# Beginning of a two-layer hybrid diffusion backbone: shift and scale in two column halves, tokens first

## What is computed

```
for l in range(DEPTH):                       # 2 layers
    mod_x = (silu(c) @ w_mod[l] + b_mod[l]); mod_c = (silu(c_ctx) @ w_mod[l] + b_mod[l])
    sh1, sc1, g1, sh2, sc2, g2 = split(mod_x, 6)          # csh1.. of mod_c alike
    hx = rms_norm(xs, norm_mix_g[l]) * (1 + sc1) + sh1;  hc = rms_norm(cs, norm_mix_g[l]) * (1 + csc1) + csh1
    oc, ox = even_mixer(hc, hx, w_in, ...) if l == 0 else odd_mixer(hc, hx, w_qkv, ...)
    xs = xs + g1 * ox;  xs = xs + g2 * sq_relu_mlp(rms_norm(xs) * (1 + sc2) + sh2, w1, w2)    # cs alike in layer 0
# even_mixer starts with h @ w_in; its first 1024 output columns are xr, which a short convolution and
# two gated scans use; then come yr, q/k/v, z and the gate columns
```

## Time and profile before

| | us |
|---|---|
| median of three runs (lowest, highest) | 1482.41 (1480.11, 1483.84) |
| the profiled execution's own time | 1480.53 |
| its span | 1478.7 |
| first product with a weight unit starts | 53.30 |

### The profile page before, as it was taken

The page is one execution under the profiler, slowest core; times in us unless marked ns, Lnnn a source line. Parts: engine busy times, 40 slices in busy tenths (PEclk is TensorE's granted clock), DMA queues, the critical chain, the costliest instruction groups (busy, mean ns, idle before and its releaser), DMA issues.

```text
span 1478.7 us, 22711 instructions
## 1 busy us (share of the span) xinstructions
PE 1400.7 (95%) x8312; PEld 1138.3 (77%) x8312; DVE 762.1 (52%) x1203; ACT 700.3 (47%) x1102; POOL 293.8 (20%) x291
## 2 busy tenths in 40 slices
PE   5799999989899999999999999999998998899998
PEld 2577777767678888877868888888887766899997
DVE  0744789875345555444364433344235545665664
ACT  2538888867434444432253421243125544554543
POOL 0100123333256666551300000000030000200001
PEclk9899999989999999999999999999999999999999
DMA  7542323221454333452323232333323320455653
GB/s 279 168 101 72 86 80 91 73 70 43 166 177 143 129 130 115 150 193 86 95 84 90 95 100 86 100 90 94 100 86 101 99 72 0 136 177 185 185 184 101
DMA packets 135695, 170.59 MB, mean 115 GB/s; under 512 B 11011, under 2 KB 122038, under 8 KB 135606
## 3 DMA queue, kind: packets, MB, share of 16 engines
q1 hardware_dynamic: 134720, 169.18, 36.4%
q10 hardware_dynamic: 886, 0.19, 0.1%
HBM read 168.30 MB, written 1.05 MB: 115 GB/s over the span
## 4 chain that ended last, share of the span: by engine, by line
PE 74%; ACT 8%; DVE 8%; issue 4%; DMA 3%; POOL 1%; ACTq 1%; SPq 0%; DVEq 0%; POOLq 0%
PE bank L1908 54%; PE bank L2208 3%; PE bank L2196 3%; PE bank L1866 2%; DMA raw<-in_w_mod 2%; ACT w_hi L779 2%; DVE w_lo L1330 2%; DVE qkv L1354 1%; PE bank L2225 1%; PE bank L2057 1%; PE bank L2150 1%; PE bank L2072 1%; POOL qkv L630 1%; PE bank L2174 1%; ACT l_i L1023 1%
## 5 line engine op out<-in xcount | busy, mean ns | idle before, releaser
L1330 DVE TENSOR_TENSOR w_lo<-raw,w_hi 128x1024 fp32r<-128x1024 f32 x216 | 269.4, 1247 | 458.7 <-ACT w_hi L779 458.6
L779 ACT ACTIVATE w_hi<-raw 128x1024 fp32r<-128x1024 f32 x216 | 228.6, 1058 | 462.5 <-PE bank L1908 458.3
L1908 PE MATMUL bank<-h_hi,w_hi 128*128 128x512 f32 (+1 forms) x1024 | 377.7, 369 | 21.1 <-ACT h_hi L967 8.0
L1908 PE MATMUL bank<-h_hi,w_lo 128*128 128x512 f32 (+1 forms) x1024 | 369.1, 361 | 0.0
L1908 PE MATMUL bank<-h_lo,w_hi 128*128 128x512 f32 (+1 forms) x1024 | 365.7, 362 | 1.2 <-DVE h_lo L1498 1.2
L1908 PEld LDWEIGHTS bank<-h_hi,w_hi 128*128 128x128 f32 x1024 | 195.0, 190 | 67.5 <-issue 23.0
L1908 PEld LDWEIGHTS bank<-h_lo,w_hi 128*128 128x128 f32 x1024 | 192.9, 190 | 36.0 <-issue 2.6
L1908 PEld LDWEIGHTS bank<-h_hi,w_lo 128*128 128x128 f32 x1024 | 194.8, 190 | 32.2
L1908 PE MATMUL bank<-hid_hi,w_hi 128*128 128x512 f32 (+1 forms) x512 | 172.8, 338 | 0.9 <-DVE w_lo L1330 0.6
L1908 PE MATMUL bank<-hid_hi,w_lo 128*128 128x512 f32 (+1 forms) x512 | 172.1, 336 | 0.0
L1908 PE MATMUL bank<-hid_lo,w_hi 128*128 128x512 f32 (+1 forms) x512 | 172.1, 336 | 0.0
(11 more groups left out here) (279 smaller groups left out, 2087.6 us busy)
## 6 DMA issues: line engine op xcount, KB each, us to landing
raw<-in_mlp_w SPq DMA_DIRECT2D x128, 512.0 KB, 3.6
raw<-in_w_mod SPq DMA_DIRECT2D x96, 512.0 KB, 4.5
raw<-in_even_w_in SPq DMA_DIRECT2D x48, 512.0 KB, 3.7
raw<-in_even_w_out SPq DMA_DIRECT2D x16, 512.0 KB, 3.4
raw<-in_attn_w_qkv SPq DMA_DIRECT2D x16, 512.0 KB, 3.5
raw<-in_attn_w_o SPq DMA_DIRECT2D x8, 512.0 KB, 3.4
xin<-in_ctx SPq DMA_DIRECT2D x1, 1024.0 KB, 9.2
xin<-in_x SPq DMA_DIRECT2D x1, 1024.0 KB, 11.3
```

The lines of the kernel that those rows point to most:

```text
L779: act.activation(w_hi[:, j % SPLIT], raw[:, j % RAW], ACT.Copy).then_inc(hi_ready, 1)
L1330: dve.tensor_tensor(w_lo[:, j % SPLIT], raw[:, j % RAW], w_hi[:, j % SPLIT].bitcast(F32), ALU.subtract).then_inc(split_done, 1)
L1908: return pe.matmul(bank[2 * pair + t][:, 0:T - n0], w[:, j % SPLIT, k, t * P:(t + 1) * P], x_[:, n0:T], start=(kk == 0 and first), stop=(k ...
```

## The change

Tokens are asked for first, in two column halves, each with its own semaphore. `w_mod` pieces of layer 0's shift and scale now hold 512 columns of shift and the same 512 of scale, so that the first eight pieces give both for feature tiles 0 to 3, the second eight for 4 to 7. They have eight slots of their own (`first_w`); the ninth and later wait on `mod_used`. Units of `xr` are asked for between them. The nineteen small loads are issued on POOL's queue. Copy, transposes, bias and gain are done per half (`half_copy`, `half_flip`, `evac_half`). PE first turns the tokens, then sums the squares with three products instead of eight (DVE adds tiles 0 to 5, `square_added`), then turns the small rows. The four first units are taken in the order pair 0, pair 1 (features 0 to 511), pair 0, pair 1 (features 512 to 1023), with the second eight pieces of `w_mod` between them. ACT writes `h_hi` itself; DVE computes gain times n_x plus shift once more in full precision (`n_y`) to get `h_lo`. POOL has no part in the first norm. DVE's softplus stands behind the norm. Of the constants, only identity, ones and epsilon come first.

```diff
@@ -520,23 +531,39 @@
 
             def load_first_mod(m):
 
-                k, col = m % KT, m // KT * MOD_COLS
-                sp.wait_ge(mod_used, m + 1)
-                sp.dma_start(raw[:, k % RAW].rearrange("p a c -> p (a c)"),
-                             a["w_mod"][0].rearrange("(k p) c -> k p c", p=P)[k][:, col:col + MOD_COLS]).then_inc(mod_in[k % RAW], 16)
+                k, col = m % KT, m // KT * (D // 2)
+                if m >= FIRST:
+                    sp.wait_ge(mod_used, PRIME_MOD + m - FIRST + 1)
+                sp.dma_start(first_w[:, m % FIRST].rearrange("p (g a) c -> p g (a c)", g=2),
+                             a["w_mod"][0].rearrange("(k p) (g c) -> k p g c", p=P, c=D)[k][:, 0:2, col:col + D // 2])\
+                  .then_inc(mod_first[m % FIRST], 16)
+
+            def load_first_unit(n):
+
+                pair, part = FIRST_PAIRS[n]
+                load_unit(w_dram["w_in"].rearrange("(h k p) c -> h p k c", p=P, k=UNIT_K)[part], n, n, pair * UNIT_C)
 
             sp.dma_start(rowsA[0:8, :], a["c_ctx"].rearrange("(k p) -> k p", p=P)).then_inc(s_c, 16)
             sp.dma_start(rowsA[8:16, :], a["c"].rearrange("a (k p) -> (a k) p", p=P)).then_inc(s_c, 16)
-            sp.dma_start(cst[:, 0:P], a["consts"][:, 0:P]).then_inc(s_c, 16)
-            for m in range(RAW):
+            sp.dma_start(cst[:, 0:N_FIRST], a["consts"][:, 0:N_FIRST]).then_inc(s_c, 16)
+            for half in range(2):
+                c_ = half * (D // 2)
+                for n, name in enumerate(("ctx", "x")):
+                    sp.dma_start(xin[:, 2 * n:2 * n + 2, c_:c_ + D // 2],
+                                 a[name][0].rearrange("(n p) d -> p n d", p=P)[:, :, c_:c_ + D // 2]).then_inc(s_x[half], 16)
+            for m in range(KT):
                 load_first_mod(m)
-            sp.dma_start(xin[:, 0:2, :], a["ctx"][0].rearrange("(n p) d -> p n d", p=P)).then_inc(s_x, 16)
-            sp.dma_start(xin[:, 2:4, :], a["x"][0].rearrange("(n p) d -> p n d", p=P)).then_inc(s_x, 16)
-            sp.dma_start(cst[:, P:N_EARLY], a["consts"][:, P:N_EARLY]).then_inc(s_ones, 16)
-            for m in range(RAW, 2 * MOD_BATCH):
+            load_first_unit(0)
+            for m in range(KT, KT + 3):
                 load_first_mod(m)
-            sp.dma_start(wg[:, :, :], w_dram["w_in"][:, 6144:6176].rearrange("(k p) c -> p k c", p=P)).then_inc(s_x, 16)
-            sp.wait_ge(mod_used, 2 * MOD_BATCH + PRIME_MOD)
+            load_first_unit(1)
+            for m in range(KT + 3, 2 * KT - 1):
+                load_first_mod(m)
+            load_first_unit(2)
+            load_first_mod(2 * KT - 1)
+            load_first_unit(3)
@@ -559,6 +586,8 @@
                                   it * (2 * UNIT_C) + (s["c0"] + pair * UNIT_C))
 
                 peeled = 0
@@ -582,11 +611,31 @@
         def _(pool):
             pool.memset(cs[:, :, 2:], 0.0).then_inc(s_cs, 1)
 
-            def first_norm():
-
-                for k in range(KT):
-                    pool.wait_ge(nrm["h"], 2 * (k + 1))
-                    pool.tensor_copy(h_hi[:, k], n_x[:, k]).then_inc(nrm["hi"], 1)
+            def rows(dst, r0, src, n):
@@ -722,7 +771,6 @@
                 glink(pool.tensor_copy(mix_hi[:, t_], xc[:, t_]))
                 pool.tensor_tensor(mix_lo[:, t_], xc[:, t_], mix_hi[:, t_].bitcast(F32), ALU.subtract).then_inc(g_x, 1)
 
-            first_norm()
             gate_parts()
             for i in range(22):
                 silu(i)
@@ -944,17 +999,21 @@
 
                 act.preload_act_table_set("natural_log_exp_and_others")
                 root("mix0", T)
-                mod_copy(0)
-
                 split_hi(0, 0)
-                split_hi(1, 1)
-                act.wait_ge(s_gain, 1)
-                for k in range(KT):
-                    act.wait_ge(nrm["t"], k + 1)
-                    for v, t0, t1 in SEGS:
-                        y_ = n_x[:, k, t0:t1]
-                        act.activation(y_, y_, ACT.Identity, bias=modv[:, 0, 0, k, v:v + 1],
-                                       scale=gain[:, 0, 0, k, v:v + 1]).then_inc(nrm["h"], 1)
+                for half in range(2):
+                    half_copy(half)
+                    act.wait_ge(s_gain, half + 1)
+                    for k in range(HALF * half, HALF * half + HALF):
+                        act.wait_ge(nrm["t"], k + 1)
+                        for v, t0, t1 in SEGS:
+                            ins = act.activation(h_hi[:, k, t0:t1], n_x[:, k, t0:t1], ACT.Identity, bias=modv[:, 0, 0, k, v:v + 1],
+                                                 scale=gain[:, 0, 0, k, v:v + 1])
+                        ins.then_inc(nrm["high"], 1)
+                        if k == KT - 2:
+                            split_hi(3, 3)
+                    if half == 0:
+                        split_hi(1, 1)
+                        split_hi(2, 2)
 
             def norm(name, layer, which, c0):
 
@@ -1458,19 +1492,53 @@
                 link(dve.scalar_tensor_tensor(out=gain[:, layer, which], in0=modv[:, layer, 3 * which + 1], scalar=1.0,
                                               in1=g_, op0=ALU.add, op1=ALU.mult))
 
+            def evac_half(half):
+
+                dve.wait_ge((half_t, mod_t)[half], 1)
+                for h in range(2):
+                    k0, k1 = HALF * half + h, HALF * half + HALF
+                    ps = bank[(X1, X2)[half]][:, h * P:h * P + P].rearrange("p (g i w) -> p g i w", g=2, i=2)[:, :, :, 0:2]
+                    b_ = V("b_mod", 0, 2 * KT).rearrange("p (g k) -> p g k", g=2)[:, :, k0:k1:2].unsqueeze(3).to_broadcast([P, 2, 2, 2])
+                    link(dve.tensor_tensor(modv[:, 0, 0:2, k0:k1:2, :], ps, b_, ALU.add))
+                k0 = HALF * half
+                g_ = V("mix_g", k0, HALF).unsqueeze(2).to_broadcast([P, HALF, 2])
+                link(dve.scalar_tensor_tensor(out=gain[:, 0, 0, k0:k0 + HALF], in0=modv[:, 0, 1, k0:k0 + HALF], scalar=1.0,
+                                              in1=g_, op0=ALU.add, op1=ALU.mult))
+                dve.sem_inc(s_gain, 1)
...
             def first_norm():
 
+                def scaled(k):
+                    dve.tensor_tensor(n_x[:, k], xT[:, k], n_rs[:, :], ALU.mult).then_inc(nrm["t"], 1)
+
+                def low(k):
+                    dve.wait_ge(nrm["t"], k + 1)
+                    for v, t0, t1 in SEGS:
+                        ins = dve.tensor_scalar(n_y[:, k, t0:t1], n_x[:, k, t0:t1], gain[:, 0, 0, k, v:v + 1],
+                                                modv[:, 0, 0, k, v:v + 1], ALU.mult, ALU.add)
+                    link(ins)
+                    dve.wait_ge(nrm["high"], k + 1)
+                    dve.tensor_tensor(h_lo[:, k], n_y[:, k], h_hi[:, k].bitcast(F32), ALU.subtract).then_inc(nrm["lo"], 1)
+
                 dve.wait_ge(nrm["rt"], 1)
-                for k in range(KT):
-                    dve.tensor_tensor(n_x[:, k], xT[:, k], n_rs[:, :], ALU.mult).then_inc(nrm["t"], 1)
-                evac_mod(0)
-                make_gain(0, 0)
-                dve.sem_inc(s_gain, 1)
+                scaled(0)
+                scaled(1)
                 split_lo(0, 0)
+                evac_half(0)
+                for k in range(HALF):
+                    low(k)
+                    if k + 2 < HALF:
+                        scaled(k + 2)
+                for k in range(HALF, KT):
+                    scaled(k)
                 split_lo(1, 1)
-                for k in range(KT):
-                    dve.wait_ge(nrm["hi"], k + 1)
-                    dve.tensor_tensor(h_lo[:, k], n_x[:, k], h_hi[:, k].bitcast(F32), ALU.subtract).then_inc(nrm["lo"], 1)
+                split_lo(2, 2)
+                evac_half(1)
+                dve.sem_inc(s_mod, 1)
+                for k in range(HALF, KT):
+                    low(k)
+                    if k == KT - 2:
+                        split_lo(3, 3)
...
+
+            def square_added(k):
+
+                dve.wait_ge(nrm["sq"], k + 1)
+                if k > 1:
+                    dve.wait_ge(s_acc, k - 1)
+                dve.tensor_tensor(n_sq[:, 0], n_sq[:, 0], n_sq[:, k], ALU.add).then_inc(s_acc, 1)
+
+            turned(1)
+            turned(3)
+            square_added(1)
+            square_added(2)
+            turned(5)
+            square_added(3)
+            square_added(4)
+            turned(7)
+            square_added(5)
...
+            first_norm()
             dve.wait_ge(s_lam, 2)
             softplus(64, 80)
             link(dve.tensor_scalar(lru_h, lru_c, -LRU_C / 2, None, ALU.mult))
             dve.tensor_scalar(lru_c, lru_c, -LRU_C, None, ALU.mult).then_inc(s_lam, 1)
-            first_norm()
...
+            def first_sum():
+
+                pe.wait_ge(s_acc, KT - 3)
+                pe.matmul(bank[X0][:, :], C("ones"), n_sq[:, 0], start=True, stop=False)
+                for k in (KT - 2, KT - 1):
+                    pe.wait_ge(nrm["sq"], k + 1)
```

(33 more changed lines are left out.)

170 lines of the change are left out of this document (97 added, 73 removed).

## The result

The changed kernel takes 1471.34 us (median of five, 1465.11 to 1474.42), the kernel before 1483.46 beside it: ratio 0.9912, 95% interval 0.9884 to 0.9941. Forecast were 1470 and a gain of 12.3; measured is 12.1. The profiled execution took 1474.42, the slowest of the five, with a span of 1472.6. The first weight product starts at 31.06 us instead of 53.30, the fifth unit at 65.94 instead of 77.2.

A forecast was written before the change was run, and what follows sets the result against it. TensorE, busy 95% of the span, was taken as the bound, so gains lie in its idle beginning: fifth unit 13.3 us earlier, less 1.0 for the clock, gain 12.3, giving 1468.2 profiled, 1470 against the median; range 1462 to 1478.

The forecast's parts named there:

- G: Time when the first half's gain is ready, at the kernel's beginning: R + 5.1 on VectorE, so 29.1 us.
- The step from G to the fifth unit: First four units of `xr`: VectorE paces, the fifth starts at G + 34.7, 63.8 us, after 3.2 us idle on TensorE.
- The small rows are the open term: Beginning: the small row loads, now issued by POOL, set the gain through R, taken as 24 us.
- R: Time when TensorE can read the small rows: 24 us, the middle between 19.5 and 28.
- lower bound: Earliest R: ACT's 18.4 us for 19 loads, counted from POOL's first free moment at 1.0, so 19.5 us.
- transposes, copies, squares and root run beneath the pieces: Beginning: with tokens landing near 8 and 10 us, this work is hidden under the `w_mod` pieces' transfers.
- The steps that I had put behind R: From the rows to the gain: 5.1 us on VectorE, 4.6 on TensorE, including 2.0 for seventh and eighth piece.
- The step on transfers: Beginning: at 405 GB/s from 7 us, the eighth piece is usable at about 20.9 us, the first weight unit at 22.2.
- Tensor-by-scalar: VectorE's `h_lo` tiles: each 256-column operation takes 0.27 us, between 0.24 and 0.49.
- The clock behind the gap: TensorE's 3.2 us idle ahead of the fifth unit costs clock speed: between 0 and 1.5 us, taken as 1.0.
- The rival in which TensorE stays at 1.2 GHz between tiles: First units: low clock while waiting for VectorE puts the fifth unit at 80.1 us, time 1485; chance 6%.
- Everything should move by the same amount: Behind the fifth unit all queues, waits and durations stay the same, so its 13.3 us earlier start carries through.

The follow-up runs named there:

- the first profile: The changed kernel as first measured, against the kernel before: 1471.34 us, ratio 0.9912; its profiled execution took 1474.42.
- the second profile: The changed kernel measured again with no edit, against the kernel before: 1467.26 us, ratio 0.9898.
- the run with tiles first: Changed kernel with TensorE turning all eight token tiles before the third piece, then two pieces, sum, rows, six pieces: 1467.25 us, ratio 0.9912 to the kernel before.

## Why the prediction was right, and where its steps were not

**The time was right, and its two main steps were right in size.** G came out at 29.73 for 29.1, the fifth unit at 65.94, 64.04 and 64.23 for 63.8. The step from G to the fifth unit was right in place too. TensorE, without a gap from 31.06, sets the second half's gain: at G + 19.6 in the first profile and 18.6 in the second, for 18.5. From there VectorE paces. Softplus stands in the 2.6 us gap ahead of the fifth unit (3.2 forecast), shown by moving it.

**But G was right for a wrong reason.** The step "The small rows are the open term" failed. R is 17.6 by the list of transfers after, 17.55 by the wait in the kernel before with that part alone, both below the "lower bound" of 19.5: I had laid ACT's whole 18.4 us over POOL's start, though POOL's issues need 0.48 to 0.68 each and rows landed 2.6 to 7.2 us after theirs, many in flight at once. Rows on ACT's queue change nothing either. The Trainium skill, DMA: Bandwidth & Descriptors (Queues, rings and completion order), says that a DMA engine takes packets from its queues in turn; by this small loads would not wait out a backlog on another queue, and I had put R near 20 by it. The 17.6 us on POOL's queue agree with it; the 10.4 us of the last load on ACT's queue, a queue of its own too, stay unexplained. Anatomy of one DMA in that page gives about 2.0 us fixed for a transfer issued by GpSimd; the first row's 2.6 us is near it, and the loads are not strung out: all 19 were over 16.3 us after the first issue.

What stood in place of R is the sentence "transposes, copies, squares and root run beneath the pieces". On their data they could; on TensorE's one queue they take turns, and the sum ended at 24.7. Had I added up that queue from its first tile, with its waits for pieces, I should have found it. So TensorE read the rows at 25.2. The steps that I had put behind R then follow: 4.5 us from there to G on VectorE, for 5.1. On TensorE's side the seventh and eighth piece took 1.07 us together, not the 2.0 taken for the half clock; VectorE's side ended later, so this cost nothing. The step on transfers was short too: 405 GB/s from 7 us on was taken from before, 346 and 332 came; the eighth piece is usable at 23.6 instead of 20.9, the first weight unit at 24.85 instead of 22.2 (seen where nothing else holds them, in the run with tiles first). Why the rate was lower is open. That pieces of 2 KB rows are slower as such is not what the later windows show: 395 GB/s from 28 to 35 us, with pieces and units in turn. What ruled, the sum at 24.7, and next the eighth piece and the first unit, happened to lie where I had put the rows, at 24: that G came out was luck.

**Tensor-by-scalar** was mis-sized: 0.73 for two, 0.37 each, for the 0.27 taken between 0.24 and 0.49. I had scaled 0.486 with columns: half the columns took three quarters of the time. Little of it counts. In the first half TensorE sets the pace; in the second three tiles make 0.6 of the 0.8 us by which the last `h_lo` came later behind the gain than forecast. The other 1.1 of the 1.5 us in the first profile lies ahead of that gain: TensorE stayed at half clock longer at the start, so that the first two pieces between the products took 1.87 us where they took 1.00 in the second profile. Softplus and what follows took 0.3 less than forecast.

**The clock behind the gap** was at the end of its 0 to 1.5: from 66.7 to 70.1 us products of the fifth unit came every 0.43 us, eight of them, 0.195 too long each: 1.5, where I took 1.0. The rival in which TensorE stays at 1.2 GHz between tiles did not come; 0.59 from 28 to 35 us is the half clock at the start, for which the sum had 1.5 us.

**"Everything should move by the same amount"** holds only on average. In the first profile the changed kernel is 11.3 us ahead at the fifth unit, 13.0 at 322 us, 8.3 at 762, 6.1 at the end; in its second 13.2, 15.5, 14.8 and 12.8. Part of the 13.0 at 322 us is chance as well: the kernel before ran at half clock for 12 us behind its stop, the changed kernel for 4.6. The losses behind 322 us go with the clock: the span's mean granted clock is 0.987 before, 0.985 in the first profile and 0.989 in the second, and of the changed kernel's 15 executions the slowest has 0.982 and the five fastest 0.989 to 0.992. That a forecast within 2 us of the median was met owes something to luck too, with single runs from 1464.8 to 1475.8.

**Without the interleaving almost nothing was left of the gain** (ratio 0.9991): tokens first, slots and the rows' queue shorten the start by 9.9 us, and the order by halves gives 9.1 of them back. But up to some 5 us of that are the place of one pair of transposes in that run, so how much of the 12 belongs to the interleaving alone, nearly all or about half, stays open.

## What to carry to other kernels

Add up each in-order engine from its first instruction before calling work "hidden beneath" transfers: what is independent in its data still stands in one queue. Where TensorE waits for transfers ahead of its first product, move duties that are not needed yet behind it: eight pieces cost 13.3 us ahead, between 1 and 5 between the units, where their transfers were over. When one duty is moved, look at what stays queued behind it: a pair of transposes left in place made VectorE wait 5.18 us. Look for the next limit within 2 or 3 us before moving work: here softplus alone and tiles alone moved the start but not the time beyond its noise, and only together, with the gain's chain ahead of the first unit, did they show.

## What the runs showed of the hardware

**Half clock behind a stop has no fixed length.** The stop near 297 us is 5.1 us in all twelve profiles without work in it. Behind it TensorE ran at half clock although it had work again: for 3 to 5 us in nine of them, 9 in one (the kernel before with rows on POOL), 12 in two (the kernel before, 310.7 to 322.7, and softplus moved). Between executions of one kernel the end moves by up to 10 us (1465.7 to 1475.8), more than most of these edits, and the slower ones have the lower mean clock. This one stop is not the main source: with work in it single runs still spread over 7.2 us.

**Transfers dip where the rows are issued by POOL.** Windows at 14 and 15 us, last column GB/s, of the changed kernel, and of the same with rows on ACT:

```profile
14.00:15.00 1.00, 1.00 (x8) 0.72 (x4) 0.00 (x0) 0.00 (x0) 0.00 (x0) 1.00 1.47 298
15.00:16.00 1.00, 1.00 (x9) 0.20 (x8) 0.00 (x0) 0.78 (x2) 0.00 (x0) 1.00 0.74 112
```

```profile
14.00:15.00 1.00, 1.00 (x7) 1.00 (x5) 0.00 (x0) 0.98 (x3) 0.00 (x0) 1.00 1.08 364
15.00:16.00 1.00, 1.00 (x10) 0.21 (x9) 0.55 (x1) 0.82 (x2) 0.00 (x0) 1.00 1.07 367
```

For about a microsecond the rate falls to between a quarter and 0.6 of itself, in eleven of the twelve profiles with the rows on POOL (114 and 171 in the kernel before with that part) and never with them on ACT. The exception is the run with four slots, with 326 and 353 GB/s, where SP's queue had less asked for. So in that profile POOL's loads alone did not make the dip; what does was not tried. It costs some 0.25 MB, under 1 us, and it is not what separates 346 GB/s from the 405 of the earlier trace rows: with the rows on ACT it was 357 from 7 to 14 us.
